# A decoder trunk block: expert-table loads on one queue, and on two

## What is computed

```python
def block(args):
    xb, idb, gb = args
    ub = jnp.take(u_tab, idb, axis=0)
    act = jax.nn.gelu(jnp.einsum('tkd,td->tk', ub, xb))
    vb = jnp.take(v_tab, idb, axis=0)
    return jnp.einsum('tk,tkd->td', gb * act, vb)
```

## Time and profile before

| | |
|---|---|
| median of 3 runs | 1807.4 us (1804.14, 1807.4, 1808.75) |
| the profiled execution, time | 1805.16 us |
| its span, first to last instruction | 1803.4 us |
| PE busy | 1733.4 us, 96% |
| DVE, ACT, POOL busy | 1070.4, 265.6, 255.4 us |
| moved by DMA | 671.94 MB, mean 373 GB/s |
| mean granted TensorE clock | 0.991 |

### The profile page before, as it was taken

One profiled execution on the slowest core, in us unless ns is written; L12 is line 12 of the kernel. 1 busy time (PEld: TensorE's weight loads), 2 busy tenths in 40 slices (PEclk: granted clock), 3 DMA queues, 4 the chain that ended last, 5 costly groups with the idle time before them and its releaser, 6 DMA issues.

```text
span 1803.4 us, 26778 instructions
## 1 busy us (share of the span) xinstructions
PE 1733.4 (96%) x11476; PEld 1648.2 (91%) x11476; DVE 1070.4 (59%) x1396; ACT 265.6 (15%) x491; POOL 255.4 (14%) x210
## 2 busy tenths in 40 slices
PE   8999999998999999999999999999999999989997
PEld 6888888877899999999988899999999999989997
DVE  6667778697699968983445544444444444434542
ACT  2003311442732121121000000000000000000002
POOL 0000000000000012211222122233121221212210
PEclk9999999999999999999999999999999999999999
DMA  9999889977666789998999999999999999999991
GB/s 390 421 420 418 355 279 420 390 262 311 260 236 249 261 253 420 420 401 302 421 422 421 422 422 422 422 421 422 418 421 420 421 420 421 421 421 421 420 390 47
DMA packets 95342, 671.94 MB, mean 373 GB/s; under 512 B 12576, under 2 KB 12992, under 8 KB 14768
## 3 DMA queue, kind: packets, MB, share of 16 engines
q1 hardware_dynamic: 53376, 383.24, 52.6%
q0 software_dynamic: 29008, 208.49, 28.3%
q10 hardware_dynamic: 12864, 78.85, 11.3%
HBM read 664.36 MB, written 6.18 MB: 372 GB/s over the span
## 4 chain that ended last, share of the span: by engine, by line
PE 59%; DMA 36%; DVE 3%; ACT 1%; SPq 0%; issue 0%; ACTq 0%; DVEq 0%
PE ps L535 32%; PE ps L818 14%; DMA vmore<-vtab 14%; DMA wraw<-wst 11%; DMA mod_first<-wmod 6%; DMA wraw<-vtab 4%; PE ps L795 2%; PE ps L525 1%; PE ps L524 1%; PE ps L526 1%; DMA gat<-utab,gidx 1%; PE ps L674 1%; PE ps L675 1%; PE ps L676 1%; DVE mod_first L1241 1%; DVE wlo L1401 0%
## 5 line engine op out<-in xcount | busy, mean ns | idle before, releaser
L535 PE MATMUL ps<-h,wraw 128*128 128x160 f32 (+1 forms) x4160 | 588.7, 301 | 17.9 <-ACT act_u L1089 7.7
L535 PEld LDWEIGHTS ps<-h,wraw 128*128 128x128 f32 x4160 | 571.7, 190 | 29.0 <-DMA wraw<-wst 11.9
L1572 DVE SCALAR_TENSOR_TENSOR yacc<-gat,pact,yacc 128x2048 f32<-128x2048 f32 x96 | 225.6, 2350 | 272.5 <-DMA gat<-vtab,gidx 272.0
L1561 DVE SCALAR_TENSOR_TENSOR gat<-gat,hrep 128x2048 f32<-128x2048 f32 x96 | 219.9, 2292 | 210.1 <-DMA gat<-utab,gidx 210.0
L818 PE MATMUL ps<-p,vmore 128*128 128x160 f32 x2048 | 287.7, 301 | 12.6 <-DMA vmore<-vtab 12.5
L818 PEld LDWEIGHTS ps<-p,vmore 128*128 128x128 f32 x2048 | 281.3, 191 | 17.6 <-DMA vmore<-vtab 17.5
L818 PE MATMUL ps<-p,wraw 128*128 128x160 f32 x2048 | 284.4, 300 | 4.1 <-DMA wraw<-vtab 4.0
L818 PEld LDWEIGHTS ps<-p,wraw 128*128 128x128 f32 x2048 | 279.3, 190 | 7.7 <-DMA wraw<-vtab 7.7
L1685 POOL DMA_INDIRECT gat<-vtab,gidx x96 | 126.7, 1320 | 431.2 <-PE ps L818 211.0
L1685 POOL DMA_INDIRECT gat<-utab,gidx x96 | 119.6, 1245 | 446.7 <-DVE gat L1561 230.1
L535 PE MATMUL ps<-hid,wraw 128*128 128x256 f32 x832 | 180.7, 379 | 0.0
(11 more groups left out here) (267 smaller groups left out, 1221.7 us busy)
## 6 DMA issues: line engine op xcount, KB each, us to landing
wraw<-wst SPq DMA_DIRECT2D x131, 1024.0 KB, 11.6
wraw<-wst ACTq DMA_DIRECT2D x71, 1024.0 KB, 8.5
mod_ring<-wmod SPq DMA_DIRECT2D x67, 1024.0 KB, 10.8
wraw<-vtab SPq DMA_DIRECT2D x64, 1024.0 KB, 30.4
vmore<-vtab SPq DMA_DIRECT2D x64, 1024.0 KB, 30.7
mod_first<-wmod SPq DMA_DIRECT2D x22, 1024.0 KB, 20.0
g_ring<-wmod SPq DMA_DIRECT2D x7, 1024.0 KB, 7.0
x<-xT SPq DMA_DIRECT2D x4, 512.0 KB, 5.3
```

The lines of the kernel that those rows point to most:

```text
L535: r = mm(ps_w[k % 2][:, 0:T - low], wraw[:, j, kk, :], src[:, kk, low:T], start=(kk == 0), stop=(kk == KD - 1))
L1561: V.scalar_tensor_tensor(gat[slot][:], gat[slot][:], 1.0, hrep[:, s_], ALU.mult, ALU.mult, accum_out=dots[:, s_, k:k + 1]).then_inc(s_used, 1)
L1572: V.scalar_tensor_tensor(yacc[:, s_], gat[slot][:], pact[:, s_, k:k + 1], yacc[:, s_], ALU.mult, ALU.add).then_inc(s_used, 1)
```

## The change

Even U and V blocks are still loaded by SP, odd ones by ScalarE. In ScalarE's program the load of U block b+4 stands in `gelu(b)` of every odd b, behind the wait for block b's product and ahead of the gelu; behind the last U block ScalarE goes on with the odd V loads, and the third set's row gelu, the three late rows and `sel_back` take places between or behind these loads. `LOWER_TAKE` goes from 188 to 190.

```diff
-LOWER_TAKE = 188
+LOWER_TAKE = 190
+ROW_GELU_AT = 47
...
+        def v_slot_free(engine, m):
+            if m < W_RING:
+                engine.wait_ge(s_wmm, N_U + NB - W_RING + m + 1)
+            elif m < V_RING:
+                engine.wait_ge(s_p0, NB // BATCH)
+            else:
+                engine.wait_ge(s_vmm, m - V_RING + 1)
...
             with sp.Fori(0, (NB - W_RING) // W_RING) as i:
-                for j in range(W_RING):
+                for j in range(0, W_RING, 2):
...
-            for m in range(NB):
-                if m < W_RING:
-                    sp.wait_ge(s_wmm, N_U + NB - W_RING + m + 1)
-                elif m < V_RING:
-                    if m == W_RING:
-                        sp.wait_ge(s_p0, NB // BATCH)
-                else:
-                    sp.wait_ge(s_vmm, m - V_RING + 1)
+            for m in range(0, NB, 2):
+                v_slot_free(sp, m)
                 sp.dma_start(v_slot(m), vnat[:, m, :]).then_inc(s_v[m % V_RING], 16)
...
+            def load_v(m):
+                act.dma_start(v_slot(m), vnat[:, m, :]).then_inc(s_v[m % V_RING], 16)
...
                 act.wait_ge(s_wmm, N_U + b + 1)
+                if b % 2 and b + W_RING < NB:
+                    load_w((N_U + b) % W_RING, N_U + b + W_RING)
+                elif b % 2:
+                    load_v(b + W_RING - NB)
                 A(act_u[:, act_slot(b), :], ps_u[b % 2], ACT.Gelu_apprx_tanh).then_inc(s_wev, 1)
...
+            def last_rows():
+                act.wait_ge(s_vmm, p0_free(133.5))
+                act.wait_ge(s_g2d, 16)
+                act.dma_start(g2row[:], gain_dram[1:2].to_broadcast([P, D])).then_inc(s_g2, 16)
+                act.dma_start(x2[:], res_dram).then_inc(s_back, 16)
+                act.dma_start(fnrow[:], fnorm.to_broadcast([P, D])).then_inc(s_fn, 16)
...
-            row_gelu(2)
-            own.did(A(unused, ones[:, 0:1], ACT.Sqrt))
+            for m in range(W_RING + 1, NB, 2):
+                v_slot_free(act, m)
+                load_v(m)
+                if m == ROW_GELU_AT:
+                    row_gelu(2)
+                    own.did(A(unused, ones[:, 0:1], ACT.Sqrt))
+                if m == p0_free(133.5) + V_RING - 1:
+                    last_rows()
```

## The result

| | before | after |
|---|---|---|
| median | 1807.4 us | 1819.46 us (1816.24 to 1822.87) |
| profiled execution: time, span | 1805.16, 1803.4 us | 1819.46, 1817.4 us |
| PE busy | 1733.4 us | 1721.2 us |
| mean granted TensorE clock | 0.991 | 0.976 |

The ratio of the times after to before is 1.0072, 95% interval 1.0053 to 1.0092: slower by 13 us by that ratio (0.0072 of 1807.4; the two medians are 12 us apart). The median lies 1.5 us above the forecast's range and 3 us above the price of the rival "the gathers' tail". TensorE is busy for 12 us less and the kernel is slower all the same.

The account below looks back on a forecast made before the run. The prediction took a full DMA pipe, about 421 GB/s shared equally among busy queues, as the bound. Output rows 3 us early and 3 us lost to the clock summed to 0, so 1807 us, range 1799 to 1818.

Parts of the forecast that it names:

- the gathers' tail: Slower rival, after the last V load: ten gathers landing at 3.4 us or more each delay the output rows; 1816, chance 0.26.
- Loads should now keep up: U and V blocks: with two queues loads may take 281 GB/s instead of 211, where TensorE asks for 240.
- the remaining 181 GB/s: Gathers' share beside two load queues: one per 5.8 us, where the schedule asks for one per 5.5 us.
- About 6 are missing: At the last weights: 22 us fewer cost 8.9 gathers, VectorE's earlier pause covers 2.8, so about 6 are still to come.
- about 1197, where the last weights end now: End of U work: last weights end no later than before, so TensorE's 22 us lead is given back there.
- With the gathers arriving a little unevenly I take 1762: Tail: take 191 ends at 1762, against 1760.5 at the earliest for VectorE; about ten gathers remain after the last load.
- I charge 2 us: V block 4: after idling 15 us TensorE restarts partly at its lower clock, costing 2 us, hence 1208.
- I take 3: First output rows: after idling 20 us TensorE starts at a lower clock, costing 3 us.
- The row gelu costs nothing: Around V block 40: ScalarE finishes it at some 1373.5, when V block 49's slot comes free at 1373.8; no cost.
- The shares do not move: Rival: load queues are often empty, so loads get no more than before; 1808 to 1809, no change, chance 0.14.
- faster, 1800: Rival, at the end: gathers close at the pipe's own rate and TensorE's restart costs little; some 1800, chance 0.18.
- signs of being wrong: Listed beforehand: loads landing as late as before, changed DMA rate, ScalarE late at row gelu, end takes over 3.4 us apart.

Follow-up runs that it names:

- e3: The change, but with all its U and V loads on ScalarE's queue and none on SP's; ratio to the kernel before 1.0005.
- e12: The change with VectorE's tail work earlier, four more tail buffers, last weights nine takes earlier, row gelu behind load 63; ratio to before 1.0056, 1816.43 us.
- e2: The change for V loads only, odd ones on ScalarE, all U loads on SP; ratio to the kernel before 1.0021.
- e8: The kernel before, with ScalarE loading only odd V blocks from 99 on, selection behind load 115, first split behind take 190; ratio to before 1.0022.
- e5: The change with the last weights behind take 87 instead of 96; ratio to the kernel before 1.0047.
- e1: The change for U loads only, V loads, row gelu and late rows as before; ratio to the kernel before 1.0052.
- e9: The change with VectorE's tail work earlier: diagonal and fill behind take 174, selection behind load 115, first split behind take 180; ratio to before 1.0046.
- e11: The change with both VectorE's tail work moved earlier and four more buffers for the last eight gathers; ratio to the kernel before 1.0027.
- e10: The change with four more buffers for the last eight gathers, in slots of V blocks 120 to 123; ratio to the kernel before 1.0055.

## Why the prediction was wrong

The bytes moved from 680 to 1780 are equal (445.8 to 446.6 thousand, as GB/s times us, in before, after, e3 and e12), so the account can be made in transfers. After 1740 before had 6.3 MB to go, after 10.16 MB: the pipe was 9.1 us behind by then. About 4.8 of that lie in two places, 2.0 in 840 to 880 (399 for 420 GB/s) and 2.9 in 1180 to 1220 (391 for 421). The rest is 1.9 in 680 to 840 (377 for 382, but e2 and e8, whose U loads stand as before, have 379 and 378), 0.7 in 1700 to 1740 (413 for 420) and 2.3 in 1220 to 1700 (419 for 421, near what whole numbers can tell).

- **"Loads should now keep up", the gathers get "the remaining 181 GB/s"**: right. In 900 to 1050 the gathers got 180 GB/s (26.95 of 63.3 MB) and the loads 242, what TensorE asks for; the two thirds that equal parts would have allowed them were not called for. TensorE's wait for U loads fell from 7.7 to 3.3 us, and U blocks ended at 1175.7 (forecast 1173).
- **"About 6 are missing" and "about 1197, where the last weights end now"**: the step that failed first. They ended at 1208.65. The sum took the pipe as full, counted the load of V block 3 alone and credited 2.8 gathers from a pause of VectorE: six gathers and one load, 7.3 MB from 1173 on. But ten takes were left at 1173. From then to 1208 the queues moved 10.9 MB of gathers and 2.6 MB of loads. With TensorE early, its loads of V blocks 0 to 3 came ahead of gathers that were late already, and then soon little but gathers was left to move, at 371 GB/s in 1180 to 1200. V block 4 began at 1219.84 (forecast 1206), and the last four V blocks at 1751.49 (forecast 1739): this lateness went through nearly unchanged.
- **"With the gathers arriving a little unevenly I take 1762"**: mis-sized, on top of the 9 us. The forecast allowed 7 us past the earliest landing, 1755. Measured, 10.16 MB from 1740 could have landed by 1764, and take 191 ended at 1778.4, 14 us past it. The ten steps from the start of take 181 to that of take 191 took 33.3 us, 3.33 each, close to the cadence that the slower rival asked for (3.4); 5.9 us of them are the diagonal, the fill and the split. The forecast had these in its earliest end, 1760.5, but with VectorE at work without a pause, and added 1.5 us for all waits. Counted along TensorE, the same 16 us look otherwise: the last V load landed at about 1745 (forecast 1731), ten takes were left as forecast, and take 191 ended 33 us behind it (forecast 31).
- **"I charge 2 us", "I take 3" for the clock**: right in size. The restart at V block 4 took 2.9 us (20.46 against 17.55), the end from the first output rows on 33.6 us against 31.3, 2.3. The late rows cost 4.28 us of waiting ahead of V block 99 (forecast 5.5).
- **The row gelu costs nothing**: right, though it came at 1402 and not 1373.5; V loads had that much in hand. e5 shows the price when they don't.
- **"The shares do not move"** was wrong, and **"faster, 1800"** as well: gathers alone didn't close at the pipe's rate. The slower rival had named a pipe that is not full at the change of tables; of the prediction's signs of being wrong, the DMA rate dropped (371 to 413 GB/s in places ahead of 1740), while takes further apart than 3.4 us just did not come.

On the page "DMA: Bandwidth & Descriptors", section "Issuing engines are not separate DMA queues", the Trainium skill says that spreading saves issue time alone. For the bytes this case agrees: 63.3 MB in 900 to 1050 with one load queue and with two, and in e3 a ratio of 1.0005 with all loads moved to another engine. The split over two queues was not neutral, 1.0072: it changes who lands first.

What is shown: two load queues, not the engine, make the loss (e1 to e3); TensorE's waits are no measure of it where TensorE has a lead or the gathers end last (e3, e5, e12), though they count where neither holds (e8); the tail's share is four buffers and VectorE's other work together (e9 to e11, 8.1 of 13). Inferred, not shown by itself: that the 4.9 us left in e11 are its stretches 840 to 880 (392 GB/s, 2.7 us) and 1180 to 1220 (383, 3.6 us). The two make 6.3, and after 1740 e11 still had 10.4 MB to go, so arrears do not pass into the time one for one: in before TensorE, not the pipe, ended last, with its last take done 30 us ahead of the first output rows. The run that would refill the second, e12, gave it back in the tail. That one load queue keeps a backlog of loads, which fill the pipe whenever gathers are held, is my reading of why before has no such gaps; queue lengths are not in the trace. No version here beats the kernel before.

## What to carry to other kernels

Where two streams share a full pipe, a stream that waits is not yet a loss: ask whether it has a lead and which stream ends last. Then ask which stream can fill the pipe alone, and keep work of that one waiting for as long as the other has gaps. Here a second queue for one stream only moved the arrears to the other, and the arrears came back where they were hardest to hide, at an order constraint and at the end. Make the account in bytes left at a late moment of both traces, and look at what the consumer of the late stream still has to do there.

## What the runs showed of the hardware

- With little but gathers left to move (9.67 of 10.16 MB), four buffers and VectorE busy for 33 of the 40 us, 254 GB/s were moved over 1740 to 1780 in after, though each gather landed in 8.0 us in the median (20.7 among the loads). In 1740 to 1760 it was 266; 339 with VectorE's other work out of the way (e9), 394 with eight buffers (e10), 402 with both (e11).
- GpSimd's issue of a gather shows as 0.94 us when VectorE is idle, and as up to 3.0 us when it starts while VectorE has an instruction under way. Of the 158 issues in after from 850 on, 28 are longer than 1 us, and all 28 start inside an instruction of VectorE; of the 130 others 127 start while VectorE is idle. Three that follow one another from 861.91 on take 0.94 each. So the slow issues in the tail go with VectorE's work and not with GpSimd's own; no run changed this by itself. The first two rows here overlap, and at 1739.80 VectorE is idle:

```profile
1716.21 2.28 DVE L1617 TENSOR_TENSOR yacc<-yacc,g2row 128x2048 f32<-128x2048 f32 x1
1716.56 2.74 POOL L1705 DMA_INDIRECT gat<-vtab,gidx  x1 [5.27 <-DVE yacc L1592]
...
1739.80 0.94 POOL L1705 DMA_INDIRECT gat<-vtab,gidx  x1 [2.87 <-DVE yacc L1592]
```

- After an idle time of 26.59 us TensorE started at the lower clock (granted 0.86 in 1220 to 1240) and lost 2.9 us; after 22.4 us at the output rows 2.3.
